# Last layer's expert rows added up in PSUM by products with a token-weight matrix

## The chip, the cores and the metric

The kernel runs on one core of one Trainium2 chip. The metric is the device time of one execution in microseconds, from the first to the last instruction and what lies around them. The kernel before takes 1517.56 us in the median of three runs (1515.45 to 1520.23).

## What is computed

The reference is a two-layer backbone over 256 latent and 256 context tokens of width 1024. Each layer has a mixer (attention, a long convolution, a gated convolution) and then a mixture of 16 experts, of which two are chosen for each token. In the last layer only the 256 latent tokens go through the experts. This part matters here:

```python
def moe(h, w_router, b_router, w_gate, w_up, w_down):
    ...
    wts = jnp.take_along_axis(s, eidx, axis=1)
    wts = wts / jnp.sum(wts, axis=-1, keepdims=True)
    combine = jnp.sum(jax.nn.one_hot(eidx, N_EXPERTS, dtype=F32) * wts[..., None], axis=1).astype(t.dtype)
    out = jnp.zeros_like(t)
    for e in range(N_EXPERTS):
        y = (jax.nn.silu(t @ w_gate[e]) * (t @ w_up[e])) @ w_down[e]
        out = out + combine[:, e:e + 1] * y
    return out.reshape(shp)
...
x = x + gt2 * moe(hx2, w_router, b_router, w_exp_gate[l], w_exp_up[l], w_exp_down[l])
```

## The kernel before

Each engine has its own block of code, and semaphores order them. A block walks through both layers; inside a layer come the mixer's weight units, the router, and the experts. All data is float32.

**Routing and rows.** Once the router has its sums, VectorE ranks the experts by their token counts and gives every (token, choice) pair a row number `rowid` in a list sorted by expert. A plan known at build time (`ExpertPlan`, lines 22 to 47) gives each rank room in chunks of 32 rows; tokens beyond it go to extra chunks from row `extra_base` on. GpSimd scatters the token rows (`trow`, 4 KB each) to `x_rows` in DRAM by four indirect DMAs (line 659), one for 128 tokens and one choice each. `x_rows` and `y_rows` have 2560 rows, are shared by both layers and are zeroed by SyncE during layer 0's mixer, in blocks of 128 rows (512 KB), two blocks with each weight unit (line 550).

**Steps of the last layer.** The plan has 18 steps, nine of 64 rows and nine of 32, and after them a loop over extra chunks of 32 rows, whose count is read at run time (it ran once in the profiled execution). The order of ranks is `(0, 7, 9, 5, 3, 3, 14, 4, 11, 2, 2, 13, 8, 1, 1, 12, 6, 10)`. The first three steps take their tokens by products with a 0/1 matrix; from step 3 on ScalarE loads the rows of a step from `x_rows` to `xpick`, three steps ahead, on its DMA queue. The engines do this for step s:

- SyncE loads the expert's weights in six loads of 1 MB (`expert_unit`), four for gate and up, two for down, into one of two slots of `wexp`. Load j waits for `used{slot}{j}`, which TensorE raises after the last product that reads that part. SyncE issues in a fixed order, so a load that waits holds up all behind it.
- TensorE: `gate_up(s)` (line 2074), transposes of the next step's rows (`step_columns(s + 1)`), `down(s - 1)` (line 2089), `turn(s)` (lines 1695 and 2104), which transposes gate and up.
- VectorE: copies `xg` and `gu_sb` out of PSUM, and `product(s)`, the product of silu and up (`act_a`).
- ScalarE: the row loads, `y_out(s - 2)`, `silu(s - 1)`.

`y_out` copies the step's result from bank 3 to `yrow` and writes it to `y_rows` in DRAM by two DMAs (64 rows) or four (32 rows):

```python
fn(yrow[:, 0:w * 8], bank[3][:, 0:w * 8], ACT.Copy).then_inc(S("y_ev"), 1)
act.wait_ge(S("y_ev"), s + 2)
for h in range(n):
    act.dma_start(y_rows[row, h * 8 * w:(h + 1) * 8 * w], yrow[h * w:(h + 1) * w, 0:w * 8]).then_inc(S("y_out"), 64 // n)
```

The first step's weights have their own early load. ScalarE begins the stage only when the scatters of `x_rows` have landed (`scattered`).

**After the last step.** VectorE waits until all of `y_rows` is written and lets GpSimd gather both rows of each token (`yg`, line 667, four indirect DMAs). For each 128 tokens ScalarE scales the first row by its weight, VectorE adds the scaled second one (`comb`), TensorE transposes the sum in eight products, and VectorE adds it, times the channel's gate, to `xT` (line 1103). ScalarE writes the output from `xT` in two halves of 128 tokens (line 1087). Layer 0 does the same for its 512 tokens, with the next layer's work beside it.

## Time and profile before

| | |
|---|---|
| median of the three timed runs | 1517.56 us |
| span of the profiled execution | 1515.9 us |
| TensorE busy, whole span | 1301.8 us (86%) |
| TensorE weight loads / VectorE / ScalarE / GpSimd busy | 823.6 / 605.5 / 411.7 / 117.9 us |
| mean granted TensorE clock | 0.912 of 2.4 GHz |
| DMA in all | 381.25 MB, mean 251 GB/s |
| last layer's experts, from their routing to the last down product | about 1211 to 1492.0 us |
| from there to the end | 1492.0 to 1515.9 us |

The profile is one execution, recorded by the hardware profiler. Times in its rows are microseconds from the start of the span unless a column says ns. A line number is that of the kernel's file; line 679 is the helper for all of ScalarE's activations, 1097, 1100 and 1103 are VectorE's, 1695 is TensorE's transpose. A matmul in float32 shows as two records. The DMA share is the mean busy share of the core's 16 DMA engines; a queue is the row of rings that one issuing engine feeds (q1 SyncE, q10 ScalarE, q0 GpSimd). "Landing" is the time from a DMA's issue to its semaphore.

### The profile page before, as it was taken

Reading aid. Unit: us, or ns where it says so; the run is one execution under the profiler, and the core shown is the slowest. Engines: PE = TensorE matmul, PEld = TensorE weight load, DVE = VectorE, ACT = ScalarE, POOL = GpSimd, SP = SyncE. Lnnn points to the kernel's source line nnn. Section 1 sums busy time; section 2 is a strip of 40 time slices with the busy share of each in tenths; the row PEclk is TensorE's granted clock in tenths of the full one; section 3 lists DMA queues with packets and bytes.
Section 4 is the critical chain, followed back from the end, with each engine's and each line's share of the span. In section 5 each row is a group of like instructions: output and inputs, shape, how many; then the busy total and the mean of one; then the engine's idle time right before and its main releaser. Section 6 shows DMA issues by size and latency. Waiting matters only on the chain.

```text
span 1515.9 us, 19883 instructions
## 1 busy us (share of the span) xinstructions
PE 1301.8 (86%) x8082; PEld 823.6 (54%) x8082; DVE 605.5 (40%) x1067; ACT 411.7 (27%) x645; POOL 117.9 (8%) x111
## 2 busy tenths in 40 slices
PE   3889999999999797999999947988899858788873
PEld 1467778777777463333343335876788733322321
DVE  0444667675462521211131145558767351101112
ACT  1432225553251400010100035336456300000000
POOL 0000000000030020000000020009702010000001
PEclk9889999999999859999999967999999869979886
DMA  9666844121310589999988844763333579999995
GB/s 382 246 264 247 332 177 186 56 102 66 111 56 30 222 318 376 393 399 357 348 335 327 315 150 175 301 254 135 135 114 142 194 288 325 392 408 387 399 422 197
DMA packets 63951, 381.25 MB, mean 251 GB/s; under 512 B 9552, under 2 KB 14356, under 8 KB 24436
## 3 DMA queue, kind: packets, MB, share of 16 engines
q1 hardware_dynamic: 45056, 338.71, 57.3%
q10 hardware_dynamic: 14708, 24.36, 4.9%
q0 software_dynamic: 4096, 16.91, 3.1%
q8 instruction: 64, 1.05, 0.3%
q14 instruction: 27, 0.22, 0.0%
HBM read 358.71 MB, written 42.21 MB: 264 GB/s over the span
## 4 chain that ended last, share of the span: by engine, by line
issue 42%; PE 38%; DVE 8%; ACT 4%; DMA 4%; POOL 3%; ACTq 0%; POOLq 0%; DVEq 0%; SPq 0%
PE bank L1729 9%; PE bank L1731 9%; PE bank L1730 9%; PE bank L1737 2%; POOL m_lo L645 2%; DMA hrow_d<-in_hy_bias 1%; DMA stage<-in_in 1%; PE bank L1994 1%; PE bank L1695 1%; DVE conv L1103 1%; DVE wlo L1097 1%; POOL x_rows L659 1%; DMA yg<-y_rows,rowid 1%; ACT L679 1%; PE bank L1745 1%
## 5 line engine op out<-in xcount | busy, mean ns | idle before, releaser
L2074 PE MATMUL bank<-wexp,xg 128*64 128x512 f32 (+1 forms) x1504 | 290.6, 638 | 54.6 <-DMA wexp<-in_expert 51.5
L1729 PE MATMUL bank<-h_hi,whi 128*128 128x512 f32 (+1 forms) x640 | 227.8, 356 | 6.6 <-DVE h_lo L1097 5.5
L1730 PE MATMUL bank<-h_lo,whi 128*128 128x512 f32 (+1 forms) x640 | 221.3, 346 | 0.0
L1731 PE MATMUL bank<-h_hi,wlo 128*128 128x512 f32 (+1 forms) x640 | 221.1, 345 | 0.0
L2074 PEld LDWEIGHTS bank<-wexp,xg 128*64 128x64 f32 (+1 forms) x1504 | 79.5, 130 | 228.1 <-issue 158.4
L1097 DVE TENSOR_TENSOR wlo<-stage,whi 128x2048 fp32r<-128x2048 f32 x56 | 132.7, 2376 | 62.5 <-ACT whi L679 61.2
L2089 PE MATMUL bank<-wexp,act_a 128*32 128x256 f32 (+1 forms) x1072 | 144.0, 491 | 6.5 <-DVE act_a L1097 6.2
L1729 PEld LDWEIGHTS bank<-h_hi,whi 128*128 128x128 f32 x640 | 125.5, 196 | 27.8 <-DVE h_lo L1097 7.8
L679 ACT ACTIVATE yrow<-bank 128x512 f32<-128x512 f32 (+1 forms) x47 | 23.8, 506 | 425.3 <-PE bank L2089 343.8
L1730 PEld LDWEIGHTS bank<-h_lo,whi 128*128 128x128 f32 x640 | 125.8, 197 | 13.3 <-issue 0.5
L1731 PEld LDWEIGHTS bank<-h_hi,wlo 128*128 128x128 f32 x640 | 125.4, 196 | 13.6
L679 ACT ACTIVATE whi<-stage 128x2048 fp32r<-128x2048 f32 x56 | 106.9, 1911 | 87.7 <-DMA stage<-in_in 44.7
L1610 DVE COPY gu_sb<-bank 128x512 f32<-128x512 f32 x47 | 32.5, 691 | 238.0 <-PE bank L2074 237.9
L1097 DVE TENSOR_TENSOR act_a<-act_s,bank 128x256 f32<-128x256 f32 (+1 forms) x47 | 17.1, 364 | 229.9 <-ACT act_s L679 229.9
L2089 PEld LDWEIGHTS bank<-wexp,act_a 128*32 128x32 f32 (+1 forms) x1072 | 48.8, 125 | 72.8 <-issue 53.2
L667 POOL DMA_INDIRECT yg<-y_rows,rowid x12 | 14.7, 1227 | 598.6 <-DVEq L1654 595.5
L1103 DVE SCALAR_TENSOR_TENSOR conv<-glu,vec,conv 128x512 f32<-128x512 f32 (+1 forms) x90 | 57.0, 680 | 0.9
L679 ACT ACT_TABLE_LOAD x43 | 55.2, 1283 | 7.2 <-issue 6.5
L679 ACT ACTIVATE act_s<-bank 128x256 f32<-128x256 f32 (+1 forms) x47 | 15.9, 338 | 139.6 <-PE bank L1695 69.3
L1737 PE MATMUL bank<-stage,cst 128*32 128x256 f32 x416 | 32.1, 433 | 21.3 <-DMA vec<-in_vec 14.6
L1729 PE MATMUL bank<-m_hi,whi 128*128 128x512 f32 (+1 forms) x128 | 45.4, 355 | 4.2 <-POOL m_lo L645 4.1
L1695 PEld LDWEIGHTS bank<-tables,xpick 64*128 64x128 f32 (+1 forms) x344 | 25.3, 142 | 36.1 <-issue 36.1
(283 smaller groups left out, 1712.4 us busy)
## 6 DMA issues: line engine op xcount, KB each, us to landing
wexp<-in_expert SPq DMA_DIRECT2D x192, 1024.0 KB, 16.1
stage<-in_in SPq DMA_DIRECT2D x40, 1024.0 KB, 5.0
stage<-in_mod SPq DMA_DIRECT2D x26, 1024.0 KB, 7.3
spare<-in_mod SPq DMA_DIRECT2D x14, 1024.0 KB, 18.1
x_rows<-in_c_zero SPq DMA_DIRECT2D x20, 512.0 KB, 7.2
y_rows<-in_c_zero SPq DMA_DIRECT2D x20, 512.0 KB, 9.3
stage<-in_out SPq DMA_DIRECT2D x8, 1024.0 KB, 5.0
raw<-in_mod SPq DMA_DIRECT2D x8, 1024.0 KB, 6.9
```

The source lines that it names most:

```text
L645: nc.gpsimd.tensor_tensor(m_lo[:, t, 0:T], merged[:, t, 0:T], m_hi[:, t, 0:T].bitcast(f32), SUB).then_inc(S("m_lo"), 1)
L679: return nc.scalar.activation(out_, in_, f, **kw)
L1097: return V.tensor_tensor(o, x, y, op)
L1103: return V.scalar_tensor_tensor(out=o, in0=x, scalar=s, in1=y, op0=op0, op1=op1)
L1610: V.tensor_copy(gu_sb[:, :], bank[0][:, :]).then_inc(S("gu_sb"), 1)
L1695: return nc.tensor.transpose(o, i, ident[0:n, 0:n])
L1729: MM(o, w[0], x_[0], start=start, stop=False)
L1730: MM(o, w[0], x_[1], start=False, stop=False)
L1731: return MM(o, w[1], x_[0], start=False, stop=stop)
L1737: ins = MM(o[g:g + 32, 0:UW], cst[:, k, :], w[:, k, :], start=(k < 4), stop=(k >= 4))
L2074: ins = MM(bank[0][g * w:(g + 1) * w, :], x_[:, 2 * j + k, :], wexp[:, z, j, c], start=(first_ == 0), stop=(last_ == 0))
L2089: ins = MM(bank[3][h * w:(h + 1) * w, 0:8 * w], a_[:, kk, :], wexp[:, z, 4 + j, c], start=(kk == 0), stop=(kk == 3))
```

## The change

In the last layer, `y_rows` is no longer written and nothing is gathered. In its place:

- GpSimd scatters, after `x_rows`, a pair (token number, weight) of 8 bytes for each (token, choice) to a new DRAM list `meta`, by four more indirect DMAs.
- ScalarE, in its step 1 and ahead of the silu of step 0, waits for these scatters and loads the pairs of all 27 chunks into SBUF by six DMAs: for 64-row steps twice (`meta_wide`), for 32-row steps four times (`meta_half`), so that the pairs lie beside every partition group of y. In the loop it loads the extra chunk's pairs by four DMAs.
- VectorE makes for each step a matrix `spread` of 128 partitions by 256 tokens: the weight where the column is the row's token, else 0. The first one waits for the six loads.
- TensorE multiplies y (as stationary operand, 128 channels at a time) with `spread` and accumulates in banks 4 to 7, `combine(s - 2)` in step s, between `down(s - 1)` and `turn(s)`: eight products of 256 columns a step, whose row groups alternate between the halves (64 rows) or quarters (32 rows) of the partitions. Four products of 512 columns with a zero operand open the banks and four close them.
- ScalarE copies y into one of two buffers and issues no DMA for it.
- VectorE adds the banks, times the gate, to `xT` in eight operations of 256 columns; the output goes out in four DMAs of two channel blocks each.

Beside this, `x_rows` becomes one list for each layer (20 and 12 blocks), so 12 more blocks of 512 KB are zeroed in layer 0, with a small one for `meta`; the constant tables grow by 264 columns; some semaphores are merged (`u_act`/`u_dve` to `u_row`, `c_silu`/`cst_zero` to `cst`) or counted over both layers.

```diff
@@ sync: zeroing in layer 0
-                        load("all", "rows_zeroed", x_rows[b * P:(b + 1) * P, :], A["c_zero"])
-                        load("all", "rows_zeroed", y_rows[b * P:(b + 1) * P, :], A["c_zero"])
+                        for rows_ in (*x_rows, y_rows):
+                            if b * P < rows_.shape[0]:
+                                load("all", "rows_zeroed", rows_[b * P:(b + 1) * P, :], A["c_zero"])
...
@@ gpsimd
+                if l == DEPTH - 1:
+                    pool.wait_ge(S("meta_ok"), 2)
+                    for t in range(T // P):
+                        for c in range(2):
+                            pool.indirect_dma_start(
+                                out=meta, out_offset=bass.IndirectOffsetOnAxis(ap=rowid[:, 2 * t + c:2 * t + c + 1], axis=0),
+                                in_=tokm[:, c, t, :], in_offset=None,
+                            ).then_inc(S("meta_in"), 16)
...
@@ scalar: y_out
+                    if l == DEPTH - 1:
+
+                        if not isinstance(s, int):
+                            act.wait_ge(S("acc"), s)
+                        elif s >= 2:
+                            act.wait_ge(S("acc"), s - 1)
+                        buf = yrow if isinstance(s, int) and s % 2 == 0 else yrow_b
+                        fn(buf[:, 0:w * 8], bank[3][:, 0:w * 8], ACT.Copy).then_inc(S("y_ev"), 1)
+                        return
...
+                def meta_windows(w):
+
+                    return bass.AP(meta.tensor, 0, [[2, w], [2 * E, CHUNKS], [1, 2]])
...
+                    if l == DEPTH - 1 and s == 1:
+
+                        act.wait_ge(S("meta_in"), 2 * NT * 16)
+                        for h in range(2):
+                            act.dma_start(meta_wide[C * h:C * h + C, :, :], meta_windows(C)).then_inc(S("meta_ld"), 16)
+                        for h in range(4):
+                            act.dma_start(meta_half[E * h:E * h + E, :, :], meta_windows(E)).then_inc(S("meta_ld"), 16)
...
@@ scalar: output
-                    for t in range(2):
-                        act.wait_ge(S("x_moe"), (t + 1) * KT)
-                        act.dma_start(out[:, :, t * P:(t + 1) * P], xT[:, :, t * P:(t + 1) * P]).then_inc(sem("all", "rows_out"), 16)
-                    act.wait_ge(sem("all", "rows_out"), 32)
+                    for j in range(0, KT, 2):
+                        act.wait_ge(S("x_moe"), j + 2)
+                        act.dma_start(out[:, j:j + 2, :], xT[:, j:j + 2, 0:SEQ]).then_inc(sem("all", "rows_out"), 16)
+                    act.wait_ge(sem("all", "rows_out"), KT // 2 * 16)
...
@@ vector
+                def weights(s, scalars, buf):
+
+                    ts(spread[:, buf, :], token[:, 0:SEQ], scalars[:, 0:1], scalars[:, 1:2], ALU.is_equal, MUL).then_inc(S("spread"), 1)
...
+                    if l == DEPTH - 1 and s >= 1:
+
+                        u = s - 1
+                        if u == 0:
+                            dve.wait_ge(S("meta_ld"), 6 * 16)
+                        if u >= 2:
+                            dve.wait_ge(S("acc"), u - 1)
+                        first_row, w_ = plan.steps[u][3:]
+                        weights(u, (meta_wide if w_ == C else meta_half)[:, first_row // E, :], u % 2)
...
+                if l == DEPTH - 1:
+                    dve.wait_ge(S("acc"), count + STEPS + 1)
+                    for k in range(KT):
+                        half = bank[4 + k // 2][:, (k % 2) * SEQ:(k % 2 + 1) * SEQ]
+                        stt(xT[:, k, 0:SEQ], half, shift(5, k, 0), xT[:, k, 0:SEQ], MUL, ADD).then_inc(S("x_moe"), 1)
...
@@ tensor
+                def bound_banks(open_):
+
+
+                    for b in range(4, 8):
+                        ins = MM(bank[b][:, :], ident[:, :], before[:, 0:1].to_broadcast([P, 512]), start=open_, stop=not open_)
+                    return ins
+
+                def combine(s, w, buf, y_, first_):
+
+                    n = P // w
+                    pe.wait_ge(S("spread"), s + 1)
+                    if first_:
+                        bound_banks(True)
+                    pe.wait_ge(S("y_ev"), s + 2)
+                    for j in range(KT // n):
+                        for h in range(n):
+                            k = h * (KT // n) + j
+                            g = slice(h * w, (h + 1) * w)
+                            ins = MM(bank[4 + k // 2][:, (k % 2) * SEQ:(k % 2 + 1) * SEQ], y_[g, j * P:(j + 1) * P], spread[g, buf, :],
+                                     start=False, stop=False)
+                    ins.then_inc(S("acc"), 1)
...
+                    elif s >= 2:
+                        combine(s - 2, plan.steps[s - 2][4], s % 2, (yrow, yrow_b)[s % 2], s == 2)
                     turn(s, plan.steps[s][4])
                 down(*step(STEPS - 1))
+                if l == DEPTH - 1:
+                    for s in range(STEPS - 2, STEPS):
+                        combine(s, plan.steps[s][4], s % 2, (yrow, yrow_b)[s % 2], False)
```

## Rows read from the trace of the kernel before

**Rows 1.** Busy time by stretch of the experts' stage, with clock and DMA.

```profile
core 0: us, PE busy (x) PEld busy (x) DVE busy (x) ACT busy (x) POOL busy (x), PEclk, DMA share, GB/s
1262.00:1300.00 38.00, 27.79 (x192) 11.15 (x192) 3.63 (x7) 2.30 (x6) 0.00 (x0) 0.91 1.00 380
...
1400.00:1450.00 50.00, 44.30 (x280) 16.49 (x280) 6.46 (x12) 3.28 (x8) 0.00 (x0) 0.89 1.02 403
1450.00:1491.60 41.60, 29.55 (x230) 10.20 (x228) 3.83 (x8) 2.30 (x6) 0.00 (x0) 0.85 0.93 384
```

**Rows 2.** Who waited for whom, 1262 to 1491.6 us (total, times, longest).

```profile
PE bank L2074 <- DMA wexp<-in_expert: 40.4, 28, 4.7
```

**Rows 3.** Landing times of the expert weight loads (tile wexp, 1262 to 1516 us).

```profile
DMA to landing us min/median/max: 7.1/18.7/27.2
```

**Rows 4.** DMA from 1262 to 1489 us: queue, packets, MB, share; issues.

```profile
q1 hardware_dynamic: 11510, 83.82, 92.5%
q10 hardware_dynamic: 4013, 6.14, 8.2%
...
y_rows<-yrow ACTq DMA_DIRECT2D x18, 128.0 KB
...
y_rows<-yrow ACTq DMA_DIRECT2D x36, 32.0 KB
```

**Rows 5.** The end in order of time (start, us, engine, line, operation).

```profile
1490.07 1.93 PE L2089 MATMUL bank<-wexp,act_a 128*32 128x256 f32 x16 [0.32 <-DMA wexp<-in_expert]
...
1492.71 1.81 ACTq L997 DMA_DIRECT2D y_rows<-yrow  x4
1495.99 0.98 POOL L667 DMA_INDIRECT yg<-y_rows,rowid  x1 [262.32 <-DVEq L1654]
...
1507.65 4.30 DVE L1103 SCALAR_TENSOR_TENSOR xT<-bank,modT,xT 128x128 f32<-128x128 f32 x16
...
1509.83 2.70 ACTq L1087 DMA_DIRECT2D out<-xT  x2
```

**Rows 6.** Products in order of time: four of 512 columns, two on halves.

```profile
38.30 3.68 PE L1783 MATMUL bank<-sq,tables 128*128 128x512 f32 x8
...
1057.51 1.13 PE L1948 MATMUL bank<-kd,q 64*128 64x512 f32 x4
```

**Rows 7.** The output's issues (ns min/median/max) and its queue, 1511 to 1515.5.

```profile
L1087 ACTq DMA_DIRECT2D out<-xT x2: 547/590/632, 1509.8 to 1512.0; - x2
...
DMA to landing us min/median/max: 3.5/3.5/3.6
...
q10 hardware_dynamic: 2080, 1.05, 75.9%
```

**Rows 8.** The stage's start in order of time.

```profile
1232.72 0.96 POOL L659 DMA_INDIRECT x_rows<-trow,rowid  x1 [0.30 <-issue]
...
1249.70 0.38 ACT L679 ACTIVATE act_s<-bank 128x256 f32<-128x256 f32 x1 [36.40 <-PE bank L1695]
...
1256.97 5.32 PE L2089 MATMUL bank<-wexp,act_a 128*64 128x512 f32 x16
```

**Rows 9.** Landing of the x_rows scatters of the last layer.

```profile
DMA to landing us min/median/max: 8.9/12.3/14.5
```

**Rows 10.** Queues from 2.3 to 3.3 us: 8 KB (q1) and 64-byte pieces (q10).

```profile
q1 hardware_dynamic: 25, 0.20, 57.3%
q10 hardware_dynamic: 24, 0.00, 1.6%
```

**Rows 11.** Busy time from 1258 to 1262 us, columns as in rows 1.

```profile
1258.00:1262.00 4.00, 4.00 (x16) 1.02 (x12) 0.00 (x0) 0.00 (x0) 0.00 (x0) 0.70 0.33 78
```

**Rows 12.** Busy time in layer 0 while the lists are zeroed.

```profile
120.00:160.00 40.00, 40.00 (x200) 31.06 (x199) 20.02 (x28) 9.28 (x13) 0.00 (x0) 1.00 0.61 237
...
200.00:240.00 40.00, 39.47 (x223) 31.52 (x216) 28.18 (x49) 19.69 (x28) 0.00 (x0) 1.00 0.71 284
```

**Rows 13.** Gate and up, down and turn of wide and narrow steps.

```profile
1425.75 7.09 PE L2074 MATMUL bank<-wexp,xg 128*64 128x512 f32 x32
...
1433.38 3.65 PE L2089 MATMUL bank<-wexp,act_a 128*64 128x512 f32 x16
...
1445.35 1.10 PE L2104 MATMUL bank<-tables,gu_sb 128*128 128x64 f32 x8
```

More of the change, by code:

```diff
@@ L320, in hybrid_backbone @@
         tables = keep("tables", [P, TABLE_COLS])
-        ident, ones, headmean, before, iota, rot, headsum, fold, first, cosT, sinT, plan_table, halves = (
+        ident, ones, headmean, before, iota, rot, headsum, fold, first, cosT, sinT, plan_table, halves, token = (
             tables[:, c:c + n] for c, n in TABLES.values())
@@ L675, in _ @@
         def _(act):
-            a = Program(act, "act_steps")
             def fn(out_, in_, f, **kw):
@@ L997, in y_out @@
                         act.dma_start(y_rows[row, h * 8 * w:(h + 1) * 8 * w], yrow[h * w:(h + 1) * w, 0:w * 8]).then_inc(S("y_out"), 64 // n)
+                def meta_windows(w):
+                    return bass.AP(meta.tensor, 0, [[2, w], [2 * E, CHUNKS], [1, 2]])
                 nc.scalar.preload_act_table(ACT.Silu)
-                act.wait_ge(S("scattered"), 2 * NT * 16)
+                act.wait_ge(sem("all", "scattered"), sum(2 * (span(i) // P) for i in range(l + 1)) * 16)
                 for s in range(PICKED[l], PICKED[l] + XR - 1):
@@ L1070, in _ @@
                     act.wait_ge(S("H_ok"), 3)
-                for t in range(NT):
-                    scale_first(t)
-                    if l < DEPTH - 1 and t >= 2:
-                        next_square(t - 2)
                 if l < DEPTH - 1:
+                    for t in range(NT):
+                        scale_first(t)
+                        if t >= 2:
+                            next_square(t - 2)
                     for t in range(NT - 2, NT):
@@ L1659, in _ @@
                         rest(l + 1, p).then_inc(S("lo"), 1)
-                for t in range(NT + 1):
+                for t in range(NT + 1 if l < DEPTH - 1 else 0):
                     if t < NT:
@@ L2167, in next_sums @@
                     ins.then_inc(S("sq_sum"), 1)
-                for t in range(NT):
+                for t in range(NT if l < DEPTH - 1 else 0):
                     pe.wait_ge(S("combined"), t + 1)
```

106 lines of the change are left out of this document (72 added, 34 removed).

## The prediction

> **What bounds the kernel now.** I read the stretches of the last layer first, because every edit that can cost or give time lies there. From 1262 to 1491.6 us, where nearly all of this layer's expert work runs, the 16 DMA engines are busy 93 to 102% of the time and TensorE has holes [rows 1]. TensorE waited 40.4 us in that time for expert weights [rows 2], and a weight load of 1 MB lands 7.1 to 27.2 us after its issue, 18.7 in the median [rows 3]. One such load goes through every 2.8 us (83.82 MB, 80 loads, in 227 us [rows 4]). So six or seven loads are queued in the median and two or three at the worst: the stage runs at the pace of the DMA engines, and TensorE can release a buffer some 7 us later than now before they run dry. Then I read the end in order of time [rows 5]: the last down product ends at 1492.0, and from there to 1515.9 nothing but a single chain runs, 23.9 us: y copied and written out, a wait for the writes, four gathers, a scaled sum of two rows, transposes, sixteen additions, the output's transfer.
>
> **The tail.** It loses the write and its wait, the four gathers, both comb operations and the transposes. What stays or comes after the down product: the copy of y (0.7 us from the product's end to the point where the DMA is now issued [rows 5]), the last combine, the four closing products, eight additions of 256 columns, the last quarter of the output. Sixteen additions of 128 columns take 4.30 us, 0.27 each [rows 5]; one of 256 columns is then between 0.27 and 0.54, I take 0.4, 3.3 in all. Four products of 128x512 took 3.68 us (eight records [rows 6]); the closing ones are of that form, 3.6. An output half lands 3.5 us after its issue [rows 7]; a quarter, in 256 pieces in place of 1024, between 2 and 3.5, I take 2.9; 0.4 follow as now. The last combine I put at 1.3 (below). Sum 0.7+1.3+3.6+0.2+3.3+2.9+0.4 = 12.4, so the tail gives 11.5 us.
>
> **Combines on TensorE.** Each step gets eight products with 256 columns; 19 steps, 9 of them 64 rows wide and 10 (the loop's one iteration with them) 32. One after another, each would take half of a 512-column product, 3.68/8 = 0.43 with drain [rows 6], 3.4 us a step and 65 in all. But two products of 512 columns that read different halves of the partitions (the scores, 64x128 on 64x512) took 1.13 us together, in place of about 1.85 [rows 6]. The combine alternates its row groups from product to product in the same way, so a wide step costs 1.9 (four pairs). For four groups of 32 no row shows it: between 0.9 and 3.4, I take 1.3, as the form is nearest to the pair. That is 9x1.9+10x1.3 = 30 us, and 3.6 for the four opening products. They stand before the turn of the next step. What hides them is TensorE's 40.4 us of waits for weights, and where it runs without waiting for some steps, the 7 us and more by which its releases are early [rows 2, 3]. Only at the end nothing hides them: the combines of steps 15, 16 and 17 (1.3+1.9+1.3) come before the last expert's products, where TensorE now waits 1.4 us for its weights. That costs 3.1 us. DVE's weight row (one operation a step) and ACT's copies wait for nothing that is late in the steady state; without that cover each would cost its 0.4 us.
>
> **y_rows writes.** Within the stage ACT no longer issues 18 writes of 128 KB and 36 of 32 KB, 3.5 of the 6.14 MB of its queue [rows 4]. That queue took 8.2% of 227 us, 18.6 us; by bytes the writes are 10.7 of it. At the weights' price (92.5% of 227 us for 83.82 MB, 2.5 us a MB) they are 8.9. As the DMA engines are the bound, all of it comes back: 9.8 us, as long as TensorE keeps up.
>
> **What is new at the stage's start.** This is the term of which I am least sure. GpSimd scatters (token, weight) pairs of 8 bytes behind the last x_rows scatter, which is issued until 1233.7 [rows 8] and lands 14.5 us after its issue [rows 9]. The four new scatters are 36 more pieces on each engine (8 and a semaphore write, four times). 36 turns from 1247.2 on end at about 1259, where the weights' queue runs empty anyway (share 0.33 from 1258 to 1262 [rows 11]). ACT waits for these scatters in its step 1, ahead of the silu of step 0, with six new loads behind that wait; now this silu runs at 1249.70 and the down product of step 0 starts at 1256.97 [rows 8], so it has 6.5 us to spare. New: 1259.8, six issues of 0.55 to 0.63 us [rows 7], silu and product 0.8, down at 1264.2 or later, 7.3 us late; and the clock will have fallen to its lower level in the gap, so the product that now takes 5.3 (share of the full clock 0.70 [rows 11]) takes up to 6.8. As this product frees the buffer for which the next load waits, and SyncE issues in order, the DMA engines stand idle for that time: cost 7.3 to 10, I take 9. For the range the term goes from 0 (the second rival) to 25 (the first).
>
> The six loads themselves are 6912 reads of 8 bytes (27 chunks for 128 partitions, twice), 432 on each engine. DVE waits for them after the product of step 1. The price of a piece lies between 10.7 ns (64 bytes: 1.6% of 16 us over 24 pieces [rows 10]) and 26 ns (512 bytes: 75.9% of 4.5 us on 16 engines over 2080 [rows 7]). Between the issue at 1260 and the weights' return at about 1269.5 there is room for 8 us of them alone on the engines: at up to 19 ns each all are through, and the wait costs nothing. I take that case, as 8 bytes are nearer to 64 than to 512; the other is the first rival.
>
> **The rest.** In layer 0 twelve more blocks of 512 KB are zeroed, where DMA engines are 61 to 71% busy and TensorE is at work without waiting [rows 12]: 0, at worst 2 us if a weight load comes late. The tables are 135 KB longer ahead of the first product: 0.3. Merged semaphores: 0.
>
> **Sum.** 1515.9 - 11.5 + 3.1 - 9.8 + 9 + 0.3 = 1507.0 for the profiled execution. The median of the three timed runs is 1517.56, 1.7 above that span (they go from 1515.45 to 1520.23); so 1508.7, and I forecast 1509. About 0.3% (4.6 us) is what a measurement here can tell from no change: faster is below 1513.0, slower above 1522.1.
>
> **Rivals.** First, the loads of the pairs meet the weights. If a piece costs over 19 ns, some are left when the weights flow again, and each then costs a turn of 0.3 us. At 26 ns some 120 are left (432 less 8 us at 26 ns), while only 12 loads of weights (9 pieces an engine each, 108) can be in flight, because DVE's wait holds TensorE before the turn of step 2 and with it the releases. The weights run dry at 1303 (1269.5 and 12 loads of 2.8), the wait ends with them, and before the next buffer is free come combine and opening products 5.5, a turn 1.1, gate and up of a wide step 7.1, half a down product 1.8 [rows 13] and 0.7 of transposes: 16 us with idle engines. Up to 58 left over are free, as their turns end by 1287, 16 us before the weights run dry; so it decides between 19 and 26 ns: 1512 to 1526, at 26 ns 1525, slower. For it: at 512 bytes the measured pace is already 26 ns. Against it: that piece carries 64 times as much. Chance 0.24.
>
> Second, the small pieces don't take turns one by one but go several at a time. Then the scatters land before 1250, ACT's silu isn't late, the loads of the pairs pass between few weight pieces, and the term of 9 is 0: 1500. The counts of 25 and 24 [rows 10] speak against it, since 128 small pieces stood ready there, but they are of one queue and of transfers with eight pieces an engine. The Trainium skill ("DMA: Bandwidth & Descriptors", Queues, rings and completion order) says just this, that an engine drains a packet of some 9 to 17 descriptors from one ring before it switches. By that rule 432 pieces are 25 to 48 turns; the trace so far disagrees for the queues it shows. Chance 0.12.
>
> Third, TensorE becomes the bound. Its waits of 40.4 us shrink to 31 when the writes are gone, and 34 us of combines and opening products must fit; where the order of experts bunches them they don't, and the writes' gain is swallowed: 1515 to 1518. Chance 0.12. Fourth, the row groups don't overlap in this form (different banks, accumulating): 65+3.6 against 31, which adds over 25 us less what slack absorbs: 1530. The scores' row speaks against it. Chance 0.08. The forecast's own case has 0.44, with 1503 to 1513 for it.
>
> **Range and chances.** 1499 to 1526 takes in the second and third rival and all of the first but its end; the fourth is left out. Faster: 0.42 of the forecast's case, 0.12, and 0.03 of the first rival, 0.57. Within 0.3%: 0.02+0.08+0.10, 0.20. Slower: 0.23.
>
> **What the profile after will show.** Tail: from the last down product to the end 12 us, no GpSimd work in it. Combine: eight products in 1.9 us where 64 rows wide, 1.3 where 32; 3.4 would be the fourth rival. y_rows: ACT's queue without the writes, the weight loads of a span nearer to each other. Start: silu of step 0 after 1260 in place of 1249.7, DMA share near zero for some 10 us around 1262, and DVE's weight row of step 0 not later than 1280; if it comes past 1290 it is the first rival, if silu runs before 1256 the second. TensorE's wait for weights should fall from 40 to under 10 us; if it is zero over long stretches while the DMA share falls below 0.9, it is the third. The prediction is wrong above all if the pieces of 8 bytes have a price outside 10 to 26 ns.

## The result and the profile after

The kernel after takes 1508.23 us in the median (1506.87 to 1509.86, four runs), the kernel before beside it 1518.1 (1515.45 to 1520.23, four runs). The ratio is 0.9938 with a 95% interval of 0.9913 to 0.9962, so the change takes away 9.9 us, 5.8 to 13.2. The forecast was 1509. The profiled execution of after has a span of 1507.7 us, against 1515.9 before. The difference of the spans, 8.2 us, is what the accounts below divide up.

| | before | after |
|---|---|---|
| span of the profiled execution, us | 1515.9 | 1507.7 |
| TensorE busy, whole span, us | 1301.8 | 1324.3 |
| silu of step 0 | 1249.70 | 1266.07 |
| down product of step 0 starts | 1256.97 | 1266.96 |
| first piece of the load that waits for it | 1261.7 | 1271.8 |
| last piece of the expert weights is through | 1489.4 | 1492.3 |
| last down product ends | 1492.0 | 1496.2 |

First the start of the stage in order of time (start, us, engine, line, operation), to be held against [rows 8].

```profile
1233.04 0.96 POOL L674 DMA_INDIRECT x_rows<-trow,rowid  x1 [0.30 <-issue]
...
1238.69 0.97 POOL L683 DMA_INDIRECT meta<-tokm,rowid  x1 [0.30 <-issue]
...
1248.83 1.91 ACTq L1005 DMA_DIRECT2D xpick<-x_rows  x3
...
1252.57 7.15 ACTq L1055 DMA_DIRECT2D meta_wide<-meta  x2
...
1259.76 6.27 ACTq L1057 DMA_DIRECT2D meta_half<-meta  x4
1266.07 0.38 ACT L701 ACTIVATE act_s<-bank 128x256 f32<-128x256 f32 x1 [52.45 <-issue]
...
1266.96 5.50 PE L2170 MATMUL bank<-wexp,act_a 128*64 128x512 f32 x16 [4.82 <-DVE act_a L1145]
...
1274.12 0.41 DVE L1148 TENSOR_SCALAR spread<-tables,meta_wide 128x256 f32<-128x256 f32 x1
```

The last of the four scatters of pairs lands at 1252.55 and ScalarE goes on at 1252.57, much earlier than forecast. But the two issues of `meta_wide` and the four of `meta_half` go on until 1266.0. An issue of this engine had cost 0.55 to 0.63 us in [rows 7]; the durations of these by tile are:

```profile
L1057 ACTq DMA_DIRECT2D meta_half<-meta x4: 561/734/4148, 1259.8 to 1265.5; - x4
L1055 ACTq DMA_DIRECT2D meta_wide<-meta x2: 670/3558/6447, 1252.6 to 1253.3; - x2
```

Two of six took 6.4 and 4.1 us (columns: min, median, max in ns). Up to 1261 us almost no pair had passed, because the row loads (`xpick`, 0.64 MB) stood ahead of them in the same queue. From 1253 to 1261 us:

```profile
q10 hardware_dynamic: 195, 0.64, 27.8%
```

The silu stands behind the six issues on ScalarE, the down product of step 0 behind the silu, and the next weight load behind that. The queues (packets, MB, share of 16 engines) from 1262 to 1268 us:

```profile
q10 hardware_dynamic: 6475, 0.05, 73.2%
q1 hardware_dynamic: 11, 0.03, 1.8%
```

These are the 8-byte pieces, with almost no weights beside them: 6475 in 6 us on 16 engines, 67 a us on each, one every 14.8 ns in the mean. The engines are busy for 73.2% of that time, so a piece takes 10.9 ns by itself; the rest is idle time between pieces. The steady state, by stretch, to be held against [rows 1]:

```profile
core 0: us, PE busy (x) PEld busy (x) DVE busy (x) ACT busy (x) POOL busy (x), PEclk, DMA share, GB/s
1262.00:1300.00 38.00, 30.92 (x210) 13.28 (x213) 5.26 (x11) 2.14 (x6) 0.00 (x0) 0.87 0.85 278
...
1400.00:1450.00 50.00, 47.13 (x370) 20.60 (x360) 8.68 (x18) 3.29 (x8) 0.00 (x0) 1.00 1.01 397
1450.00:1491.60 41.60, 37.08 (x312) 17.60 (x308) 5.12 (x12) 2.90 (x7) 0.00 (x0) 1.00 0.98 403
```

The DMA share is 0.85 where it was 1.00, by the gap in the weights from 1262.8 to 1271.8, and 0.98 to 1.01 later, as before. So the DMA engines remain the bound of the stage. TensorE is busier (47.1 of 50 us in place of 44.3). Its waits for weights answer to [rows 2]:

```profile
PE bank L2155 <- DMA wexp<-in_expert: 18.0, 16, 2.3
```

The end in order of time, to be held against [rows 5]. TensorE waits for no weights in it:

```profile
1482.11 2.00 PE L2191 MATMUL bank<-spread,yrow 64*128 64x256 f32 x16
...
1484.04 1.15 PE L2191 MATMUL bank<-spread,yrow_b 32*128 32x256 f32 x16
...
1486.28 3.64 PE L2155 MATMUL bank<-wexp,xg 128*32 128x512 f32 x32 [0.59 <-DVE xg L1661]
...
1492.60 3.59 PE L2170 MATMUL bank<-wexp,act_a 128*32 128x256 f32 x32 [0.75 <-DVE act_a L1145]
...
1496.27 0.38 ACT L701 ACTIVATE yrow_b<-bank 128x256 f32<-128x256 f32 x1 [4.04 <-PE bank L2170]
1496.70 1.15 PE L2191 MATMUL bank<-spread,yrow_b 32*128 32x256 f32 x16 [0.51 <-ACT yrow_b L701]
1497.78 3.71 PE L2177 MATMUL bank<-tables 128*128 128x512 f32 x8
1501.53 3.22 DVE L1151 SCALAR_TENSOR_TENSOR xT<-bank,modT,xT 128x256 f32<-128x256 f32 x8 [7.73 <-PE bank L2177]
1502.44 2.73 ACTq L1135 DMA_DIRECT2D out<-xT  x4
```

From the end of the last down product at 1496.2 to 1507.7 there are 11.5 us, where there were 23.9. A combine of a wide step takes 2.00 us, of a narrow one 1.15, and GpSimd has no part in it.

### The profile page after: what moved, and what is told of

It is laid out like the page before. It is cut to its first block, busy times and chain, and to the rows that moved or that the text cites. A ratio compares the mean times of both kernels' runs of the same rounds, so it can differ in the third digit from the quotient of the medians.

```text
span 1507.7 us, 20479 instructions
## 1 busy us (share of the span) xinstructions
PE 1324.3 (88%) x8386; PEld 844.7 (56%) x8386; DVE 608.1 (40%) x1078; ACT 409.8 (27%) x643; POOL 118.0 (8%) x111
## 4 chain that ended last, share of the span: by engine, by line
PE 45%; issue 25%; DMA 13%; DVE 7%; ACT 5%; POOL 3%; ACTq 1%; SPq 1%; DVEq 0%; POOLq 0%
PE bank L1811 9%; PE bank L1813 9%; PE bank L1812 9%; DMA wexp<-in_expert 7%; PE bank L2155 3%; PE bank L2170 3%; PE bank L1819 2%; PE bank L1777 2%; POOL m_lo L660 2%; DMA stage<-in_in 2%; DMA hrow_d<-in_hy_bias 1%; DMA raw<-in_mod 1%; ACT L701 1%; DVE wlo L1145 1%; PE bank L2075 1%
## 5 line engine op out<-in xcount | busy, mean ns | idle before, releaser
L2155 PE MATMUL bank<-wexp,xg 128*64 128x512 f32 (+1 forms) x1504 | 283.3, 624 | 31.1 <-DMA wexp<-in_expert 28.3
L2170 PE MATMUL bank<-wexp,act_a 128*32 128x256 f32 (+1 forms) x1072 | 141.4, 482 | 10.1 <-DVE act_a L1145 10.1
L701 ACT ACTIVATE yrow<-bank 128x512 f32<-128x512 f32 (+1 forms) x37 | 19.1, 517 | 316.1 <-PE bank L2170 283.7
L1777 PEld LDWEIGHTS bank<-tables,xpick 64*128 64x128 f32 (+1 forms) x344 | 25.6, 143 | 36.7 <-issue 36.7
L1151 DVE SCALAR_TENSOR_TENSOR xT<-bank,modT,xT 128x256 f32<-128x256 f32 (+1 forms) x64 | 22.7, 409 | 55.4 <-PE bank L1813 46.1
```

Of the source, the lines that this page charges most:

```text
L701: return nc.scalar.activation(out_, in_, f, **kw)
L1151: return V.scalar_tensor_tensor(out=o, in0=x, scalar=s, in1=y, op0=op0, op1=op1)
L1777: return nc.tensor.transpose(o, i, ident[0:n, 0:n])
L2155: ins = MM(bank[0][g * w:(g + 1) * w, :], x_[:, 2 * j + k, :], wexp[:, z, j, c], start=(first_ == 0), stop=(last_ == 0))
L2170: ins = MM(bank[3][h * w:(h + 1) * w, 0:8 * w], a_[:, kk, :], wexp[:, z, 4 + j, c], start=(kk == 0), stop=(kk == 3))
```

## The experiments

The times below are medians. The runs fall into three groups (after once more, the writes, the later loads and the packed pairs; the same row group, the short products, one list and everything together; twice the pairs and the last two combinations), each with its own runs of the kernel before beside it (1518.6, 1518.0 and 1517.6 us), and a ratio is against these. Ratios and medians don't always give the same difference; where they are far apart, both are given. What comes ahead of the stage differs between executions: the first expert load is issued at 1223.0 us in the profile of after, and at 1221.1 to 1227.5 in those below. So spans are also compared from that issue on; the kernel before has 293.3 us from there to its end (1222.65 to 1515.9) and after 284.8.

**After once more**, beside the three experiments that follow.

> The changed kernel once more, as the mark for the other runs of this call. Both theories: 9 to 10 us under the kernel before (ratio 0.993 to 0.995), span about 1508.

Measured: 1507.43 us, ratio 0.9911 (0.9893 to 0.9929); 281.9 us from the first expert load, so two executions of the same kernel differ by 2.9 us in this stretch. Its silu of step 0 comes at 1269.01, 43.7 us after that load's issue; in the first profile of after it was 43.1, in that of before 27.0. The late silu is no accident of one profile.

**The writes put back.** ScalarE writes `y_rows` again, and VectorE waits for the writes at the end.

```diff
+                        if not isinstance(s, int) or s >= 1:
+                            act.wait_ge(S("y_out"), s * 64)
                         fn(buf[:, 0:w * 8], bank[3][:, 0:w * 8], ACT.Copy).then_inc(S("y_ev"), 1)
+                        act.wait_ge(S("y_ev"), s + 2)
+                        for h in range(n):
+                            act.dma_start(y_rows[row, h * 8 * w:(h + 1) * 8 * w], buf[h * w:(h + 1) * w, 0:w * 8]).then_inc(S("y_out"), 64 // n)
...
+                if l == DEPTH - 1:
+                    dve.wait_ge(S("y_out"), (count + STEPS) * 64)
```

> The changed kernel, with the rows of y written to DRAM again in the last layer, by the same DMAs as before; nobody reads them. Theory 1 (the stage runs at the pace of the DMA engines, so 3.5 MB of writes cost their engine time): 7 to 10 us slower than the changed kernel, span 1515 to 1518, and the weight loads of the stage again take about 228 us from the first after the gap to the last. Theory 2 (TensorE has become the bound with its combines, so the writes were gone for nothing): within 2 us of the changed kernel.

Measured: 1521.91 us, ratio 1.0029 (1.0009 to 1.0048), 14.5 us over after, more than either theory had. From the first piece of the load that waited for the first down product to the last piece of the weights it takes 226.8 us (1276.1 to 1502.9), at a DMA share of 0.99 to 1.02; in the run of after beside it 219.5 (1274.5 to 1494.0). So the writes cost the DMA engines 7.3 us in this pair. The same stretch takes 217.7 to 220.5 us in the ten profiles of kernels without the writes, leaving out the one with the 8-byte loads behind the silu, whose weights stop in between, and 227.7 and 226.8 in the two with them: 8.3 us by the means. The other half of the 14.5 us is not their bandwidth. A row of ScalarE near the end, with the step's copy of y, and the combine behind it:

```profile
1498.33 0.38 ACT L701 ACTIVATE yrow_b<-bank 128x256 f32<-128x256 f32 x1 [6.75 <-DMA y_rows<-yrow]
...
1498.86 1.15 PE L2198 MATMUL bank<-spread,yrow_b 32*128 32x256 f32 x16 [3.03 <-ACT yrow_b L701]
```

This kernel's copy waits until all earlier writes have landed, and the combine, and with it the last expert's products, wait for the copy. TensorE stood still for 3.0 us, and then its gate and up products took 6.20 us at a granted clock of 0.58, in place of 3.64. From the last piece of the weights to the end it has 21.1 us, after 13.2. Thus 7.3 for the traffic, 7.9 for what follows from this wait at the end and 1.6 for the later return of the weights are the 16.8 us between the two spans (1524.0 and 1507.2).

**The loads of the pairs behind the silu of step 0.** Only their place on ScalarE changes.

```diff
-                    if l == DEPTH - 1 and s == 1:
-                        act.wait_ge(S("meta_in"), 2 * NT * 16)
-                        ...six loads
                     if s > 1:
                         act.wait_ge(S("act_a"), s - 1)
                     silu(s - 1, places[s - 1][1])
+                    if l == DEPTH - 1 and s == 1:
+                        act.wait_ge(S("meta_in"), 2 * NT * 16)
+                        ...six loads
```

> The changed kernel, with ScalarE's six loads of the pairs, and their wait, moved from ahead of the silu of step 0 to right behind it. Theory 1 (the late down product of step 0 comes only from ScalarE being held while it issues the six loads, 13.5 us): the silu runs at about 1253, down 0 at about 1262 in place of 1267, and the kernel is 4 to 6 us faster than the changed one (span 1502 to 1504). Theory 2 (pieces of 8 bytes that are still queued when the weights return take turns with them one by one, about 0.3 us each): VectorE's first weight row comes after 1285 in place of 1274, and the kernel is 0 to 10 us slower than the changed one.

Measured: 1511.38 us (1501.53 to 1527.11 in 12 runs, a far wider spread than that of any other kernel here), ratio 0.9957 (0.9927 to 0.9987), so 4 us over after by the medians and 7 by the ratios. The profiled execution (1508.38) is one of its fast ones. ScalarE in it, and the next down product on TensorE:

```profile
1255.39 0.38 ACT L701 ACTIVATE act_s<-bank 128x256 f32<-128x256 f32 x1 [38.83 <-issue]
1255.80 7.00 ACTq L1070 DMA_DIRECT2D meta_wide<-meta  x2
...
1262.83 21.76 ACTq L1072 DMA_DIRECT2D meta_half<-meta  x4
...
1285.13 0.27 ACT L701 ACTIVATE act_s<-bank 128x128 f32<-128x128 f32 x1
...
1285.77 3.64 PE L2170 MATMUL bank<-wexp,act_a 128*32 128x256 f32 x32 [15.01 <-DVE act_a L1145]
```

The silu is in time and the gap at 1268 is gone: weights flow again from 1265.9. But now the 8-byte pieces meet them. The queues from 1270 to 1280 us:

```profile
q1 hardware_dynamic: 553, 4.05, 99.2%
q10 hardware_dynamic: 548, 0.00, 3.5%
```

The engines pass one piece of the pairs for each piece of the weights' queue, so a pair costs a turn of 0.29 us (548 on 16 engines in 10 us) however small it is. Four issues take 21.8 us, the silu of step 1 comes at 1285.1, and VectorE's first matrix at 1286.3 (after: 1274.1). TensorE stands still for 15 us and releases no buffer, and the weights' queue does run dry: no piece of a weight passes from 1283.8 to 1288.9. This is the mechanism of the first rival, which after itself escapes only because its pieces pass in a gap. Moving the loads gives back at least what it wins: one gap of 9.0 us has become turns beside the weights and a gap of 5.1.

**Packed pairs.** The list is laid out by place (32 places by 48 chunks), so that a partition reads one piece of 216 bytes in place of 27 of 8.

```diff
-out_offset=bass.IndirectOffsetOnAxis(ap=rowid[:, 2 * t + c:2 * t + c + 1], axis=0),
+out_offset=bass.IndirectOffsetOnAxis(ap=place_i[:, c, t:t + 1], axis=0),
...
-return bass.AP(meta.tensor, 0, [[2, w], [2 * E, CHUNKS], [1, 2]])
+return bass.AP(meta.tensor, 2 * first_, [[2 * CH, E], [1, 2 * CHUNKS]])
```

VectorE works out `place_i` in five small operations, and eight loads of 32 pieces take the place of the six.

> The changed kernel with the list of pairs laid out in DRAM by place in the chunk first, then chunk, so that a partition's 27 pairs are one piece of 216 bytes: eight loads with 32 pieces each in place of six with 6912 in all, in the same place in ScalarE's order. Theory 1 (ScalarE is held because its queue can't take so many pieces): eight issues of about 0.55 us, silu of step 0 at about 1257, down 0 right behind TensorE's products of step 2's rows at about 1262, 4 to 6 us faster than the changed kernel. Theory 2 (it is held because the row loads ahead in the queue move slowly beside the weights, whatever the number of pieces): silu still after 1262, within 2 us of the changed kernel.

Measured: 1501.77 us, ratio 0.9886 (0.9862 to 0.9910), 5.7 us less than after beside it by the medians and 3.8 by the ratios, whose intervals overlap a little; 274.0 us from the first expert load, 7.9 less. Its rows:

```profile
1250.94 1.76 ACTq L1059 DMA_DIRECT2D meta_half<-meta  x4
1252.73 2.80 ACTq L1061 DMA_DIRECT2D meta_wide<-meta  x4
1255.58 0.38 ACT L705 ACTIVATE act_s<-bank 128x256 f32<-128x256 f32 x1 [43.71 <-issue]
```

and its busy times, clock and DMA share in the stretch that follows:

```profile
1262.00:1300.00 38.00, 34.35 (x250) 14.92 (x248) 5.26 (x12) 2.31 (x6) 0.00 (x0) 1.00 1.01 396
```

The wait for the scatters and the three row loads ahead are the same, yet eight issues take 4.6 us where six took 13.5, and the DMA share from 1262 to 1300 is 1.01 where it was 0.85. So the number of pieces held ScalarE, not the wait for the scatters nor the row loads by themselves.

**Twice the pairs.** The six loads are issued twice, the second set to tiles that nothing reads.

```diff
+                        for h in range(2):
+                            act.dma_start(wide_2[C * h:C * h + C, :, :], meta_windows(C)).then_inc(S("meta_ld"), 16)
+                        for h in range(4):
+                            act.dma_start(half_2[E * h:E * h + E, :, :], meta_windows(E)).then_inc(S("meta_ld"), 16)
```

> The kernel after with the six loads of pairs issued twice ahead of the silu of step 0, the second set to tiles that nothing reads: 13824 pieces of 8 bytes in place of 6912, and VectorE's first matrix waits for all. Theory 1 (ScalarE is held at the issue for as long as the pieces take to pass, and 6912 of them need 6.6 us on idle engines): the silu comes 6 to 8 us later than in after, the DMA engines' gap around 1270 grows by as much, 1514 to 1516. Theory 2 (ScalarE is held by the turns of its three row loads beside weights, and the pairs pass beside idle time): the silu comes 3.5 us later, by the six issues alone, and the kernel by no more than 3.5 us, 1508 to 1511.

Measured: 1511.61 us, ratio 0.9971 (0.9951 to 0.9991), 3.4 to 4.2 us over the two medians of after, 5.0 to 9.1 by the ratios. Its issues:

```profile
1251.01 7.25 ACTq L1057 DMA_DIRECT2D meta_wide<-meta  x2
1258.29 6.10 ACTq L1059 DMA_DIRECT2D meta_half<-meta  x4
1264.42 1.87 ACTq L1061 DMA_DIRECT2D wide<-meta  x2
1266.32 3.18 ACTq L1063 DMA_DIRECT2D half<-meta  x4
```

The first set takes 13.4 us and the second 5.1, so the silu comes 48.5 us after the first expert load in place of 43.1 and 43.7. That lies between the two theories (3.5, and 6 to 8). Each fits a part: as long as row loads and pieces share the engines with weights, the queue empties slowly and an issue takes up to 6.5 us; once the weights are through, six issues with 6912 pieces take 5.1, a little less than the 6.4 us (432 on each engine by 14.8 ns) in which the pieces pass.

**Combine with the same row group twice or four times running.**

```diff
-                    for j in range(KT // n):
-                        for h in range(n):
+                    for h in range(n):
+                        for j in range(KT // n):
```

> The kernel after, with the two loops of the combine exchanged, so that the products which follow one another read the same row group (half or quarter of the partitions) and the group changes once or three times a step. Theory 1 (products overlap because neighbours read different row groups): eight products take 3.4 us in wide and in narrow steps in place of 2.0 and 1.15, some 35 us more TensorE work in the stage. 18 us of waits for weights hide about half of it, and nothing hides the combines of steps 15 to 18 (about 8 us): 8 to 20 us over the kernel after, 1516 to 1528. Theory 2 (the products are short because they have 256 columns and few rows, whatever their order): 2.0 and 1.15 us as now, 0 us.

Measured: 1508.12 us, ratio 0.9941 (0.9920 to 0.9963). By the medians it is within 1 us of after; by the ratios 4.6 us over the second set of runs of after and 0.5 over the first, with an uncertainty of some 4, so a small cost can't be ruled out. Both theories are missed. Its combines near the end:

```profile
1483.67 2.96 PE L2191 MATMUL bank<-spread,yrow 64*128 64x256 f32 x16
1486.56 1.17 PE L2191 MATMUL bank<-spread,yrow_b 32*128 32x256 f32 x16
```

**Short opening and closing products.** They are made of a bf16 tile of zeros.

```diff
-ins = MM(bank[b][:, :], ident[:, :], before[:, 0:1].to_broadcast([P, 512]), start=open_, stop=not open_)
+ins = MM(bank[b][:, :], zero_b[:, :], zero_b[:, 0:1].to_broadcast([P, 512]), start=open_, stop=not open_)
```

> The kernel after, with the four opening and the four closing products of 512 columns made of a bf16 tile of zeros in place of the f32 identity and an f32 zero column. Theory 1 (they are on the chain of the end at their full price): they take about 1 us in place of 3.7, the stretch from the last down product's end to the end of the span falls from 11.5 to about 8.8 us, and the kernel by 2.7 us, 1504 to 1505. Theory 2 (the last quarter of the output, or the additions, set the end whatever the closing products take): the closing products shorten, and the end comes less than 1 us sooner.

Measured: 1507.15 us, ratio 0.9923 (0.9901 to 0.9946). The timing can't tell it from after, and so doesn't show the gain that was expected. The rows of its end:

```profile
1501.74 0.82 PE L2180 MATMUL bank<-zero_b 128*128 128x512 bf16 x3 [0.16 <-issue]
1502.59 3.23 DVE L1152 SCALAR_TENSOR_TENSOR xT<-bank,modT,xT 128x256 f32<-128x256 f32 x8 [4.30 <-PE bank L2180]
```

The weight load starts at 1501.51 and the additions at 1502.59, 1.1 us in place of the 3.75 from 1497.78 to 1501.53 in after. From the last down product to the end it has 8.9 us in place of 11.5, as the first theory has it.

**One list of rows for both layers**, as in the kernel before.

```diff
-x_rows = [nc.dram_tensor(f"x_rows{l}", (ROWS[l], D), f32, kind="Internal").ap() for l in range(DEPTH)]
+x_rows = [nc.dram_tensor("x_rows0", (ROWS[0], D), f32, kind="Internal").ap()] * DEPTH
```

> The kernel after, with x_rows shared between the layers again as in the kernel before, so that 12 blocks of 512 KB fewer are zeroed in layer 0. Theory 1 (the zeroing lies beside TensorE work that doesn't wait): 0 us, within 1.5 either way. Theory 2 (it delays weight loads of layer 0): 2 to 4 us faster than the kernel after, and the last layer's stage starts that much sooner.

Measured: 1506.16 us, ratio 0.9922 (0.9898 to 0.9946), inside what can't be told from nothing. Its first expert load is issued at 1223.8, within the spread of the others.

**Everything together**: packed pairs, their loads behind the silu, short products, one list. The edits are those above.

> The kernel after with four changes together: pairs packed by place, so that they load in pieces of 216 bytes in place of 8; their loads behind the silu of step 0; opening and closing products of bf16 zeros; one x_rows list for both layers. If the parts add up: 5.7 us for the packing, as measured, 2.7 for the short closing products, 0 to 1 for the silu that no longer waits for the scatters (it came at 1255.6 with packing, 1249.7 before the change, and six us of that were spare), 0 for the list: 8 to 10 us less than the kernel after, 1497 to 1499. If the DMA engines were no longer the bound once the gap at the start is closed (TensorE at work with hardly a wait), the packing and the silu would give no more than together 6, and 1499 to 1501.

Measured: 1492.79 us (1487.32 to 1496.48), ratio 0.9834 (0.9807 to 0.9860). That beats both kernels, and the expectation by 4 to 6 us. Its profile has 271.0 us from the first expert load, only 3.0 less than the packed kernel, which is the closing products. The missing part had to be sought in the two other combinations, **packed with the loads behind the silu** and **packed with the short products**; their edits are the same lines.

> The kernel after with the pairs packed (pieces of 216 bytes) and their loads behind the silu of step 0, opening and closing products as they are. Packing alone gave 1501.8, all four changes together 1492.8, 9 us less, while the trace shows only 3 of them (the closing products). Theory A (in packing alone the silu of step 0 still waits for the scatters and is late in many executions, more than in its profile): this kernel loses that wait, 1495 to 1497. Theory B (the silu's place gives nothing once the pieces are few, and the 9 us were mostly the spread of what comes ahead of the stage): 1499 to 1502.

> The kernel after with the pairs packed, their loads ahead of the silu of step 0 as in after, and the short opening and closing products. Theory A (the wait for the scatters ahead of the silu costs some 5 us): 1498 to 1500, the packed kernel less 3 us. Theory B: the same as the kernel with packing and the later loads, within 3 us, less the closing products' 3.

| ratio to before (median, us) | loads ahead of the silu | behind it |
|---|---|---|
| packed | 0.9886 (1501.8) | 0.9858 (1496.3) |
| packed, short products | 0.9878 (1498.4) | 0.9834 (1492.8), with one list |

Both rows say the same: the loads behind the silu give 4 to 7 us in the timed runs (5.5 and 5.6 by the medians, 4.2 and 6.7 by the ratios), each with an uncertainty of some 5, and the second row has the one list as well. The profiles don't show it: from the first expert load they have 274.0 and 274.5 us in the first row, 272.0 and 271.0 in the second. Where the loads are ahead of the silu, the profiled execution took 4.7 and 2.7 us less than the median of the timed runs, where they are behind it, 1.5 and 1.4 us more. The profiles also differ in where the granted clock was low. With the loads behind, the gate and up products of step 0 took 10.0 and 10.1 us, the down product came at 1260.4 and 1260.3 and took 3.65; with the loads ahead, these products took 8.5, the down product came at 1256.5 and 1257.1 and took 6.5. This hides what the silu's place is worth. The timed runs speak for theory A, a wait for the scatters that is short in the executions that were profiled and longer in others. No trace shows it at work, so it is inferred, not shown.

## Why the prediction was right

The time was right, 1509 against 1508.2, with 8.9 us of gain on the profile's own scale against 8.2. The terms, each read between the same two points in both profiles:

| | forecast, us | measured, us |
|---|---|---|
| ahead of the first expert load | +0.3 | +0.3 |
| from there to the weights' return behind the first down product | +9 | +9.7 |
| `y_rows` writes (weights' return to their last piece: 227.7 to 220.5) | -9.8 | -7.2 |
| combines, from the last piece of the weights to the end of the last down product (2.6 to 3.9) | +3.1 | +1.3 |
| tail (23.9 to 11.5) | -11.5 | -12.4 |
| sum (of unrounded values) | -8.9 | -8.2 |

**The tail** was read rightly from the chain. The parts are 0.5 for the copy (forecast 0.7), 1.1 for the combine (1.3), 3.7 for the closing products (3.6), 0.9 until the first quarters can go, and 5.3 from the first output issue to the end. The eight additions take 3.22 us (3.3). The estimate missed that the quarters are issued while the additions still run.

**The start** has the right size for a partly wrong reason, and this is the step that failed. The prediction let the four scatters take 36 turns of 0.3 us and land at 1259.8; they landed by 1252.6, 12.4 to 13.9 us after their issue, like those of `x_rows` (9.0 to 15.8 here). The row of GpSimd's queue (q0) from 1249 to 1252.6 us shows how little was left of them:

```profile
q1 hardware_dynamic: 129, 0.96, 90.2%
q0 software_dynamic: 29, 0.00, 0.6%
```

and the landing of the four, by tile:

```profile
DMA to landing us min/median/max: 12.4/13.0/13.9
```

The second rival's condition was thus fulfilled for that queue: the trace has no pieces of 8 bytes for these scatters but 64 packets of 64 bytes, which is one for each of 4 scatters and 16 engines, with eight pairs in each. The pairs did not go piece by piece. The Trainium skill ("DMA: Bandwidth & Descriptors", Queues, rings and completion order) has an engine drain a whole packet of descriptors from one ring before it switches; the landing times and packets of GpSimd's queue agree with it. For ScalarE's queue beside that of the weights the trace disagrees: 548 and 553 packets, one for one, in the run with the loads behind the silu. The rival's time, 1500, did not come, since the second step failed the other way: six issues at 0.55 to 0.63 us are 3.5 us, and they took 13.5. The prediction took the price of an output's issue, with little ahead of it in the queue, for issues of 864 and 1728 pieces behind row loads that were still under way; that a long queue holds the issuing engine was not in the sum. The packed kernel (4.6 us for eight) shows that the number of pieces is the cause, and the doubled one agrees. Two errors, the scatters 7 us too late and the issues 10 us too short, cancelled but for 3 us, by which silu and down product are later than forecast (1266.07 and 1266.96 against 1263 and 1264.2).

**The price of an 8-byte piece** decided over the first rival. It was bounded by 10.7 and 26 ns, with 19 as the point from which weights are delayed, and the pieces came 14.8 ns apart by the queue's row, of which 10.9 are their own. All pieces were through at 1268, the weights came back at 1271.8, and VectorE's first matrix at 1274.1 waited for nothing of theirs. The run with the loads behind the silu shows that the rival's turn was right where weights flow: 0.29 us for each, and the weights dry for 5.1 us. So what decides is whether the pieces meet weights, more than the price of a piece by itself.

**The writes** brought 7.2 us between the two profiles and 7.3 where they were put back, less than the 9.8. By the means of all profiles it is 8.3 for 3.5 MB, 2.4 us a MB, which is close to the 2.5 at which weights pass (8.9 in the prediction). So bytes at the weights' price were about right, and the queue's share (10.7) put it too high.

**The combines** were right in size (2.00 and 1.15, forecast 1.9 and 1.3), and right in that nothing hides them at the end, yet they cost less there. From 1478 us on TensorE waits for no weights in after, while before it waited 1.03 and 0.32 us. The three combines from 1477.3 us on, 4.3 us in all (forecast 4.5), stand in its chain, and the last down product starts at 1492.60, when its input `act_a` is ready. What limits their cost is the last weights, which landed at 1492.8. Without the combines the second half of the product would have waited for them and ended, by an estimate, at 1494.6 (half of 3.59 us later), so they cost 1.6 us of the 4.3 here. In the kernel before it did wait:

```profile
1488.40 1.35 PE L2089 MATMUL bank<-wexp,act_a 128*32 128x256 f32 x16 [0.75 <-DVE act_a L1097]
```

This is the first half of before's last down product; the row of 1490.07 in [rows 5] is the other half, 1.93 us for half the work at a granted clock of 0.50. In after the whole product took 3.59 us at 0.53, in the second profile of after 1.93 at 1.00:

```profile
1493.69 1.93 PE L2170 MATMUL bank<-wexp,act_a 128*32 128x256 f32 x32 [0.75 <-DVE act_a L1145]
```

There the term is -1.0 us in place of +1.3, so how the clock falls at the end decides its sign, and the +1.3 is not a price of the combines. TensorE still waits 18.0 us for weights, where under 10 was forecast. The sum of busy time had been made at the old clock; now the granted clock is 1.00 in three of the four stretches from 1300 on (0.86 from 1350 to 1400), where it was 0.89 and 0.85 in the last two before [rows 1], and the same products take less time. The third rival did not come true, as the share stays at 1.01; the fourth neither, by the 2.00 us and by the reordered run, in which 8.6 us more work cost little, if anything.

**The rest**, the longer zeroing and tables, gave what was forecast: nothing that can be told apart.

## What to carry to other kernels

Count the pieces of a DMA, not its bytes, and look at what stands behind its issue on the same engine: 6912 pieces of 8 bytes held ScalarE for 13.5 us and the weights' pipeline for 10, and laying the list out so that each partition reads one piece took most of it away (4.6 us, and a DMA share of 1.01 in that stretch). In a stage that runs at the pace of the DMA engines, work can be moved to TensorE where it waits, though not into its last steps, where the waits have ended, and most of the engines' time for each MB that is no longer written comes back. Where two terms of a sum are large and of unlike certainty, read both points of each in the profile after, because a right total can rest on two errors that cancel.

## What was not expected of the hardware

- An issue on ScalarE's queue took 0.3 to 0.7 us with few pieces ahead of it (one of the packed loads 1.2), and 4.1, 6.4, up to 13.1 us (in the four that took 21.8) when thousands stood there.
- Beside weights in another queue the engines passed 8-byte pieces and 8 KB pieces one for one (548 and 553 packets in 10 us). GpSimd's scatter of the same pairs went in packets of 64 bytes.
- Eight f32 products of 32 rows and 256 columns on four row groups take 1.15 us, and 1.17 when two on the same group follow one another; on two groups of 64 rows it is 2.00, and 2.96 when four follow one another. The Trainium skill ("TensorE: Matmul & The Clock Gate", Measured speedup vs the span model) gives 3.07 times for four row groups, measured with 512 columns. One after another the eight would take 3.4 us, an estimate from the four products of 512 columns in [rows 6], 3.0 times the 1.15, which agrees.
- TensorE's granted clock was higher in most of the stage: 0.89 of 2.4 GHz from 1400 to 1450 us before, with 44.3 of 50 us busy, and 1.00, its upper level, with 47.1 busy in after. In the last down product of after, from 1492.6 to 1496.2 us, it was 0.53, near the lower level of 1.2 GHz. TensorE had been busy 3.0 of the 4.6 us ahead of it, but so it had in the second profile of after, where the clock stayed at 1.00 and the product took 1.93 us. What decides between the two stays open.
- The kernel with 8-byte loads amid weights spread over 25.6 us in 12 executions. The doubled one, whose pieces pass in the gap, spread over 11.3 in 12, and the one with packed loads behind the silu over 3.8, though in four executions only.
